# A two-block transformer kernel: the inputs of the RWKV scan made inside the attention's block and in the scan's first rounds, with sigmoids from exponential, plus one and reciprocal

## The chip, the cores and the metric

One core of one Trainium2 chip. The metric is the device time of one execution, in microseconds (us).

## The reference

The program runs two transformer blocks over 512 tokens of width 1024. The change touches the mixer of the first block. Its input projection gives queries, keys and values of eight attention heads and, after a token shift, `zr`: receptance, key and value of eight RWKV heads (64 wide each) and three low-rank inputs `xw`, `xa`, `xg`. The RWKV part computes:

```
kk = hs(k * k_k)
kk = kk * lax.rsqrt(jnp.maximum(jnp.sum(kk * kk, axis=-1, keepdims=True), 1e-12))
for direction in range(2):
    w = -softplus(-(w_decay0[direction] + jnp.tanh(xw) @ w_decay_up[direction])) - 0.5
    decay = jnp.exp(-jnp.exp(w))
    a = sigmoid(a_gate0[direction] + xa @ a_gate_up[direction])
    k_dir = k * (1.0 + (a - 1.0) * k_a)
    ys.append(wkv7_scan(hs(r), hs(decay), hs(k_dir), hs(v), kk, hs(a), reverse=(direction == 1)))
```

With s = sigmoid(w_decay0 + tanh(xw) @ w_decay_up) the decay is exp(-exp(-0.5) s), so the kernel keeps s itself, and two sigmoids are wanted for each direction: s (the "decays", tile `decay_sig`) and a (the "rates", tile `a`). The scan is a recurrence over the tokens. A product-key expert layer, a second mixer and a second expert layer follow; they are not changed.

## The kernel before, in words

Each stage is one block of programs, one for each engine, and all engines meet between blocks. The stages around the change are, in order: `stage_shifted` (projection and token shift), `stage_attention` (L687), `stage_rwkv_inputs` (L1005), `stage_rwkv_scan` (L1081) and `stage_rwkv_output` (L1515). Everything is f32, and the order of work on each engine is written out by hand; waits are on semaphore counts.

**Attention.** There are 32 units u: two heads by four tiles of 128 queries for each of four pairs of heads. TensorE makes scores for two units at a time (L730), VectorE adds a bias that SyncE streams from memory (L792) and takes the row maximum of the unit before (L795), ScalarE raises (L816) and copies the transposed probabilities (L808), TensorE transposes (`turn`, L739) and multiplies by the values (`mix`, L749). Four score tiles go round, so VectorE can be up to four units ahead of TensorE's transposes. After every eight units VectorE scales the rows (`scale`, L783 and L785), TensorE turns them back (L757) and ScalarE stores them (L812). GpSimd has nothing to do. Bank 7 of the accumulation memory is used by `turn_out` alone.

**Inputs.** In a block of its own: VectorE multiplies the keys (L1068), ScalarE squares them (L1039), TensorE sums them over each head (L1055), VectorE clamps (L1075). TensorE makes 16 products, one for each (direction d, pair of heads f, decay or rate), over 128 rows of which 64 are zero (L1062), and ScalarE evaluates Sigmoid straight from the bank (L1043). At the end ScalarE takes a logarithm (L1046) and an exponential (L1049) for the inverse root, and VectorE scales the keys (L1078).

**Scan.** There are eight rounds n; round n takes the pair of heads n // 2, forwards when n is even and backwards when it is odd. A round begins with four transposes (`turn`, L1377, copied by ScalarE at L1341) and five products (`gram`, L1389), then inverts triangular matrices in five levels l (`level` on VectorE, L1214; `z_products` and `w_products` on TensorE, L1406 and L1408; copies on ScalarE, L1349 to L1354), and ends with `end_products` and `gains` (L1247). Between these stand the 14 half steps of the recurrence of the round before (`chain`) and its output products. VectorE prepares round n + 1 in the levels of round n, one `prelude` part after each level (L1166 to L1191). In round 0 there is no chain; VectorE and GpSimd first copy unit matrices (L1262, L1266, L1310).

Of the kernel before, what the change touches and what calls it, by code (L numbers as in the profile page):

```python
# [25 lines left out]
P = 128  # L26
# [660 lines left out]
def stage_attention(core, qk, v, att):  # L687
# [9 lines left out]
    with ExitStack() as st:  # L697
        bias = core.sb("att_bias", [P, BIASES, TT, S], ctx=st)
# [11 lines left out]
        with nc.Block() as block:  # L710
            @block.sync
            def _(sp):
                core.clear_used(sp)
                for h in range(HEADS):
                    if h >= BIASES:
                        before = h - BIASES
                        sp.wait_ge(biased, PAIR * (before // 2) + PAIR - 1 + before % 2)
                    sp.dma_start(bias[:, h % BIASES, :, :], core.dram["att_bias"][h, :, :, :]).then_inc(bias_loaded[h % BIASES], 16)
                for j in range(BIASES):
                    sp.wait_ge(bias_loaded[j], 16 * len(range(j, HEADS, BIASES)))  # L720

            @block.tensor
            def _(pe):
# [28 lines left out]
                def turn_out(p):  # L752
                    pe.wait_ge(scaled, p + 1)
                    if p >= 1:
# [7 lines left out]
                for g in range(len(GROUPS)):  # L762
                    for h in range(2):
# [4 lines left out]
                        if u >= 2:  # L768
                            mix(u - 2)
                    if g % TT == 2 and g >= TT:  # L770
# [6 lines left out]
            def _(dve):  # L777
# [8 lines left out]

                for u, (h, i) in enumerate(UNITS):
# [5 lines left out]
                    if u >= 1:  # L793
                        dve.wait_ge(biased, u)
                        dve.tensor_reduce(top[:, u - 1:u], score[:, (u - 1) % SCORES, :], AX.X, ALU.max, negate=True).then_inc(topped, 1)  # L795
                    if u % PAIR == 3 and u >= PAIR:
# [6 lines left out]
            def _(act):  # L803
# [9 lines left out]

                for u in range(N):
# [3 lines left out]
                    if u >= 1:  # L818
                        copy_turned(u - 1)
                    if u % PAIR == 6 and u >= PAIR:  # L820
                        store(u // PAIR - 1)
                copy_turned(N - 1)
                store(HEADS // 2 - 1)
# [50 lines left out]
def first_block(core, first, mixed):  # L874
    with ExitStack() as st:
        zr = core.sb("zr", [P, 14, S], ctx=st)
        with ExitStack() as s2:
# [9 lines left out]
            stage_attention(core, qk, v, mixed)  # L887
        stage_rwkv(core, zr, mixed)
# [100 lines left out]
def stage_rwkv(core, zr, mixed):  # L989


    nc = core.nc
    R, K, V = 0, 4, 8
    with ExitStack() as st:
        sig = core.sb("decay_sig", [P, 8, S], ctx=st)
        a = core.sb("a", [P, 8, S], ctx=st)
        kk = core.sb("kk", [P, 4, S], ctx=st)
        sel = core.sb("rwkv_cols", [P, 4, 6], ctx=st)
        restart = core.sb("restart", [P, S], ctx=st)
        stage_rwkv_inputs(core, zr, sig, a, kk, sel, restart)  # L1000
        stage_rwkv_scan(core, zr, sig, a, kk, sel, restart, mixed)
        stage_rwkv_output(core, zr, a, sel, mixed)


def stage_rwkv_inputs(core, zr, sig, a, kk, sel, restart):  # L1005

    nc = core.nc
    with ExitStack() as st:

        lora = core.sb("lora", [P, 2, 2 * S], ctx=st)  # L1010
        low = core.sb("low", [P, S], ctx=st)
        sq = core.sb("kk_sq", [P, 4, S], ctx=st)
        lora_zeroed, loaded, restart_loaded, squashed, bank_full, emptied, made, squared, kk_full, clamped, logged, inverted = core.sems(
            st, "lora_zeroed", "lora_loaded", "restart_loaded", "squashed", "bank_full", "emptied", "kk_made", "squared", "kk_full", "clamped", "logged",
            "inverted")
        UNITS = [(d, f, which) for d in range(2) for f in range(4) for which in range(2)]
        NB = 4
        with nc.Block() as block:
            @block.sync
            def _(sp):  # L1020
                core.clear_used(sp)
                sp.dma_start(lora[0:HD, 0, :], core.dram["decay_up"]).then_inc(loaded, 16)
# [2468 lines left out]
```

## Time and profile before

| | |
|---|---|
| time, median of 3 runs | 2838.0 us (2835.01 to 2838.73) |
| the profiled execution's own time | 2833.37 us |
| its span | 2831.6 us |
| TensorE busy | 2392.0 us (84%) |
| VectorE busy | 1559.2 us (55%) |
| ScalarE busy | 982.1 us (35%) |
| attention | 259.4 to 338.4 us of the span |
| inputs of the scan | 338.7 to 368.6 us |
| scan | 368.9 to about 622 us |

Times in rows count from the start of the span. PE is TensorE, PEld its weight loads, DVE VectorE, ACT ScalarE, POOL GpSimd, SP SyncE (a name with q is the engine's sequencer). An f32 matmul is recorded as two, so one 128x128x512 product is "x2".

### The profile page before, as it was taken

How to read it: one execution, taken by the hardware profiler on the slowest of the kernel's cores; microseconds unless marked ns; L12 is line 12 of the kernel's file. 1: busy time of each engine (PE TensorE's matmuls, PEld its weight loads, DVE VectorE, ACT ScalarE, POOL GpSimd, SP SyncE). 2: the span in 40 equal slices, each digit the busy share in tenths (PEclk: the TensorE clock that was granted, in tenths of full speed). 3: DMA queues.
4: the chain of work that ended last, by engine and by line, in shares of the span. 5: the costliest groups of instructions: out<-in, count | busy, mean ns of one | idle time of the engine just before them, and what ended most of it. 6: DMA issues, size and time to landing. Idle time of an engine off the chain costs nothing. (4 is left out here: it accounts for less than half of the span.)

```text
span 2831.6 us, 45663 instructions
## 1 busy us (share of the span) xinstructions
PE 2392.0 (84%) x17210; PEld 1377.7 (49%) x17210; DVE 1559.2 (55%) x3601; ACT 982.1 (35%) x2559; POOL 927.2 (33%) x757
## 2 busy tenths in 40 slices
PE   6998979988899997777777777777779979889996
PEld 3544679985645443322233232322248878643333
DVE  6665555544666666666676766766554463420002
ACT  2121643324333333332333333333244332443333
POOL 0000021003244444555545555555520152223331
PEclk9999989998999999999999999999999966889998
DMA  9942100003499999999999999999942310379994
GB/s 374 375 166 96 59 13 4 5 4 123 181 398 398 385 384 410 421 421 419 418 416 414 415 416 411 419 409 416 417 180 82 119 39 2 125 285 357 376 355 172
DMA packets 174636, 770.15 MB, mean 272 GB/s; under 512 B 33728, under 2 KB 51792, under 8 KB 95056
## 3 DMA queue, kind: packets, MB, share of 16 engines
q0 software_dynamic: 87552, 545.34, 47.5%
q1 hardware_dynamic: 68176, 183.94, 17.5%
q10 hardware_dynamic: 18688, 37.95, 3.7%
q8 instruction: 137, 2.24, 0.3%
q14 instruction: 83, 0.68, 0.1%
HBM read 815.37 MB, written 16.78 MB: 294 GB/s over the span
## 5 line engine op out<-in xcount | busy, mean ns | idle before, releaser
L2126 PE MATMUL bank<-expert_rows,diagonals 128*128 128x512 f32 x1656 | 783.1, 611 | 210.3 <-ACT diagonals L2018 209.6
L1912 POOL DMA_INDIRECT expert_rows<-in_uv,expert_idx x414 | 533.6, 1289 | 576.8 <-PE bank L2126 476.2
L1947 DVE SCALAR_TENSOR_TENSOR expert_rows<-expert_rows,h_rows 128x1024 f32<-128x1024 f32 x414 | 507.4, 1225 | 343.6 <-DMA expert_rows<-in_uv,expert_idx 343.6
L2126 PEld LDWEIGHTS bank<-expert_rows,diagonals 128*128 128x128 f32 x1656 | 302.0, 192 | 639.1 <-ACT diagonals L2018 345.8
L2007 ACT ACTIVATE expert_act<-expert_dot 128x2 f32<-128x2 f32 x256 | 52.0, 203 | 865.4 <-DVE expert_rows L1947 662.2
L2126 PE MATMUL bank<-weight_slots,diagonals 128*128 128x512 f32 x392 | 180.8, 604 | 59.0 <-ACT diagonals L2018 59.0
L2018 ACT ACTIVATE diagonals<-ident,expert_weight 128x128 f32<-128x128 f32 x512 | 173.5, 386 | 0.0
L1947 DVE SCALAR_TENSOR_TENSOR weight_slots<-weight_slots,h_rows 128x1024 f32<-128x1024 f32 x98 | 120.1, 1225 | 89.6 <-DMA weight_slots<-in_uv,expert_idx 87.2
L1912 POOL DMA_INDIRECT weight_slots<-in_uv,expert_idx x98 | 132.6, 1354 | 109.4 <-issue 62.0
L594 DVE TENSOR_TENSOR w_lo<-weight_slots,w_hi 128x384 fp32r<-128x384 f32 (+3 forms) x120 | 80.7, 678 | 129.4 <-ACT w_hi L545 129.1
L2126 PEld LDWEIGHTS bank<-weight_slots,diagonals 128*128 128x128 f32 x392 | 70.6, 189 | 167.1 <-ACT diagonals L2018 89.8
L662 PE MATMUL bank<-rhs_hi,w_lo 128*128 128x512 f32 (+1 forms) x312 | 127.1, 407 | 23.2 <-DVE w_lo L594 15.2
L3448 DVE TENSOR_TENSOR hidden<-hidden,bank 128x256 f32<-128x256 f32 x24 | 10.1, 421 | 243.8 <-ACT hidden L3305 243.8
L2012 ACT ACTIVATE expert_weight<-expert_act,expert_gate 128x1 f32<-128x1 f32 x512 | 122.8, 287 | 8.6
L662 PE MATMUL bank<-rhs_lo,w_hi 128*128 128x512 f32 (+1 forms) x312 | 123.9, 397 | 0.0
L662 PE MATMUL bank<-rhs_hi,w_hi 128*128 128x512 f32 (+1 forms) x312 | 123.8, 397 | 0.0
L545 ACT ACTIVATE w_hi<-weight_slots 128x384 fp32r<-128x384 f32 (+3 forms) x120 | 63.5, 531 | 147.3 <-PE bank L662 145.9
L1030 POOL MEMSET lora<- 64x1024 f32 x1 | 0.9, 946 | 338.2 <-POOLq L710 338.2
L3206 PE MATMUL bank<-expert_w,tokens_turned 128*64 128x512 f32 x448 | 105.9, 608 | 0.7 <-ACT tokens_turned L3299 0.7
L925 PE MATMUL bank<-mixed,weight_slots 128*128 128x512 f32 x224 | 102.0, 611 | 0.6 <-PEq L405 0.3
L2069 PE MATMUL bank<-mixed,weight_slots 128*128 128x384 f32 x256 | 98.0, 489 | 0.0
L313 DVE SCALAR_TENSOR_TENSOR mod_acc<-mod_w,cond,mod_acc 128x512 f32<-128x512 f32 x144 | 97.4, 745 | 0.0
(531 smaller groups left out, 3974.3 us busy)
## 6 DMA issues: line engine op xcount, KB each, us to landing
expert_w<-in_experts SPq DMA_DIRECT2D x55, 1024.0 KB
expert_w_more<-in_experts SPq DMA_DIRECT2D x41, 1024.0 KB
mod_w<-in_ada_w ACTq DMA_DIRECT2D x17, 2048.0 KB, 11.8
mod_w<-in_ada_w SPq DMA_DIRECT2D x7, 2048.0 KB, 16.1
weight_slots<-in_w_in SPq DMA_DIRECT2D x6, 2048.0 KB, 17.9
weight_slots<-in_w_in SPq DMA_DIRECT2D x8, 1536.0 KB, 6.6
att_bias<-in_att_bias SPq DMA_DIRECT2D x8, 1024.0 KB, 6.2
weight_slots<-in_w_out SPq DMA_DIRECT2D x4, 2048.0 KB, 8.6
```

Source lines behind the costliest of these rows:

```text
L313: dve.scalar_tensor_tensor(out=a, in0=w, scalar=c, in1=a, op0=ALU.mult, op1=ALU.add).then_inc(self.weighed, 1)
L545: act.activation(w_hi[:, c % CH, 0:w.shape[2]], w[:, k, :], ACT.Copy).then_inc(w_upper, 1)
L594: dve.tensor_tensor(w_lo[:, c % CH, 0:w.shape[2]], w[:, k, :], w_hi[:, c % CH, 0:w.shape[2]].bitcast(F32), ALU.subtract).then_inc(w_split, 1)
L662: mm = pe.matmul(out, a, b, start=k == 0 and j == 0, stop=k == KD - 1 and j == 2)
L925: mm = pe.matmul(core.bank[u % NB][:, :], w[:, k, (u % 4) * P:(u % 4) * P + P], h[:, k, :], start=k == 0, stop=k == KD - 1)
L1912: pool.indirect_dma_start(rows[j], None, core.dram["uv"], bass.IndirectOffsetOnAxis(idx[:, t, column:column + 1], 0)).then_inc(arrived[j], 16)
L1947: dve.scalar_tensor_tensor(out=u, in0=u, scalar=1.0, in1=hN[:, t, :], op0=ALU.mult, op1=ALU.mult, accum_out=dot[:, j:j + 1]).then_inc(dott ...
L2012: act.activation(weight[:, j + i:j + i + 1], act_out[:, j + i:j + i + 1], ACT.Identity, scale=gates[:, t, column + i:column + i + 1]).then ...
L2018: act.activation(diag[:, j + i, :], core.ident[:, :], ACT.Identity, scale=weight[:, j + i:j + i + 1]).then_inc(diagonal, 1)
L2069: return pe.matmul(unit_bank(u)[:, 0:S - P], w[:, k, f * P:f * P + P], h2[:, k, P:S], start=k == 0, stop=k == KD - 1)
L2126: mm = pe.matmul(bank[2 * (t % 2) + half][:, :], diag[:, j, :], rows[slot_of(n)][:, D + half * S:D + half * S + S], start=column == 0, sto ...
L3206: mm = pe.matmul(gate_up_bank[n % 2][mine(half), :], tok[:, n % 2, k, mine(half)], both[half][:, k % HALF * S:k % HALF * S + S], start=k = ...
```

## The change

`stage_rwkv` and `stage_rwkv_inputs` are gone. A class `RwkvInputs` holds their tiles through attention and scan and gives each engine a few instructions to place between its own. The bias tiles of the attention lie in the slots of the weight ring, which are free there.

- In attention: before the first unit, keys, squares and the low-rank inputs (`first_on_vector`, `first_on_scalar`), beside three more loads on SyncE. At units 1 to 4 TensorE sums a square into bank 7, and VectorE clamps it at the unit after. At units 5 to 12 TensorE makes the eight products of pairs 0 and 1 into the same bank, one a unit, now over 64 rows with nothing to zero, and ScalarE raises each (exp of minus the sum) one unit later. At units 8 to 15 VectorE finishes the four of pair 0: plus one on even, reciprocal on odd ones. ScalarE takes the logarithm before its last store.
- In the scan: ScalarE begins with the four inverse roots, VectorE scales the keys (`norm_key`) around the unit matrices. In round 0 TensorE puts the other eight products behind the transposes (three behind the first, then two, two and one) and ScalarE raises them. In rounds 0, 2 and 4 VectorE has, after each of levels 0 to 3, one plus-one and one reciprocal of 128x512 (`squash`), for the next pair of heads.

```diff
...
     return evac
-def stage_attention(core, qk, v, att):
+def stage_attention(core, qk, v, att, rw):
...
     with ExitStack() as st:
-        bias = core.sb("att_bias", [P, BIASES, TT, S], ctx=st)
+        lent = core.ring.slots[:, :, :].rearrange("p r n -> p (r n)")
+        bias = lent[:, 0:BIASES * TT * S].rearrange("p (b i t) -> p b i t", b=BIASES, i=TT)
         score = core.sb("score", [P, SCORES, S], ctx=st)
...
                     sp.dma_start(bias[:, h % BIASES, :, :], core.dram["att_bias"][h, :, :, :]).then_inc(bias_loaded[h % BIASES], 16)
+                    if h == BIASES - 1:
+                        rw.load(sp)
                 for j in range(BIASES):
                     sp.wait_ge(bias_loaded[j], 16 * len(range(j, HEADS, BIASES)))
+                rw.all_loaded(sp)
             @block.tensor
...
                     pe.wait_ge(scaled, p + 1)
+                    if p == 0:
+                        pe.wait_ge(rw.raised, len(rw.EARLY))
                     if p >= 1:
...
                             mix(u - 2)
+                        rw.on_tensor(pe, u)
                     if g % TT == 2 and g >= TT:
...
+                rw.first_on_vector(dve)
                 for u, (h, i) in enumerate(UNITS):
...
                         dve.tensor_reduce(top[:, u - 1:u], score[:, (u - 1) % SCORES, :], AX.X, ALU.max, negate=True).then_inc(topped, 1)
+                    rw.on_vector(dve, u)
                     if u % PAIR == 3 and u >= PAIR:
...
+                rw.first_on_scalar(act)
                 for u in range(N):
...
                         copy_turned(u - 1)
+                    rw.on_scalar(act, u)
                     if u % PAIR == 6 and u >= PAIR:
...
                 copy_turned(N - 1)
+                rw.last_on_scalar(act)
                 store(HEADS // 2 - 1)
...
 def first_block(core, first, mixed):
-    with ExitStack() as st:
+    with ExitStack() as st, ExitStack() as held:
         zr = core.sb("zr", [P, 14, S], ctx=st)
...
                 stage_shifted(core, first + 3, h, zr, qk, m)
-            stage_attention(core, qk, v, mixed)
-        stage_rwkv(core, zr, mixed)
+            rw = RwkvInputs(core, held, zr, mixed)
+            stage_attention(core, qk, v, mixed, rw)
+        stage_rwkv_scan(core, zr, rw, mixed)
+        stage_rwkv_output(core, zr, rw.a, rw.sel, mixed)
...
+class RwkvInputs:
+    EARLY = [(d, 0, which) for d in range(2) for which in range(2)] + [(d, 1, which) for d in range(2) for which in range(2)]
+    LATE = [(d, f, which) for f in (2, 3) for d in range(2) for which in range(2)]
+    PAIRS, KK_AT, UNIT_AT, SIGMOID_AT = 4, 1, 5, 8
+    BANK, LATE_BANKS = 7, (4, 5, 6)
+    def __init__(self, core, st, zr, mixed):
+        self.core, self.zr = core, zr
...
+        self.low, self.sq = core.root, mixed[:, 4:8, :]
...
+    def product(self, pe, ps, unit):
+        d, f, which = unit
+        half = slice(HD * which, HD * which + HD)
+        at = d * S + f * P
+        return pe.matmul(ps[:, :], self.lora[half, at:at + P], self.low[half, :], start=True, stop=True)
+    def raise_unit(self, act, ps, unit):
+        d, f, which = unit
+        at = 8 * which + 4 * d + f
+        return act.activation(self.dest(unit), ps[:, :], ACT.Exp, scale=-1.0, bias=self.neg[:, at:at + 1])
+    def add_one(self, dve, unit):
+        return dve.tensor_scalar(self.dest(unit), self.dest(unit), 1.0, None, ALU.add)
+    def invert(self, dve, unit):
+        return dve.reciprocal(self.dest(unit), self.dest(unit))
+    def first_on_scalar(self, act):
+        act.activation(self.low[0:HD, :], self.zr[0:HD, 12, :], ACT.Tanh).then_inc(self.squashed, 1)
+        act.activation(self.low[HD:P, :], self.zr[HD:P, 12, :], ACT.Copy).then_inc(self.squashed, 1)
+        for f in range(4):
+            act.wait_ge(self.made, f + 1)
+            act.activation(self.sq[:, f, :], self.kk[:, f, :], ACT.Square).then_inc(self.squared, 1)
+    def first_on_vector(self, dve):
+        core, sel = self.core, self.sel
+        for f in range(4):
+            dve.tensor_scalar(self.kk[:, f, :], self.zr[:, 4 + f, :], core.col("k_k", f), None, ALU.mult).then_inc(self.made, 1)
+        dve.tensor_scalar(self.neg[:, :], core.col("w_decay0", 0, 16), -1.0, None, ALU.mult).then_inc(self.negated, 1)
...
+    def on_tensor(self, pe, u):
+        ps = self.core.bank[self.BANK]
+        f, i = u - self.KK_AT, u - self.UNIT_AT
+        if 0 <= f < 4:
+            pe.wait_ge(self.squared, f + 1)
+            if f >= 1:
+                pe.wait_ge(self.clamped, f)
+            pe.matmul(ps[:, :], self.core.headones[:, :], self.sq[:, f, :], start=True, stop=True).then_inc(self.kk_full, 1)
+        if 0 <= i < len(self.EARLY):
+            if i == 0:
+                pe.wait_ge(self.clamped, 4)
+                pe.wait_ge(self.loaded, 32)
+                pe.wait_ge(self.squashed, 2)
+            else:
+                pe.wait_ge(self.raised, i)
+            self.product(pe, ps, self.EARLY[i]).then_inc(self.unit_full, 1)
+    def on_scalar(self, act, u):
+        i = u - self.UNIT_AT - 1
+        if 0 <= i < len(self.EARLY):
+            if i == 0:
+                act.wait_ge(self.negated, 1)
+            act.wait_ge(self.unit_full, i + 1)
+            self.raise_unit(act, self.core.bank[self.BANK], self.EARLY[i]).then_inc(self.raised, 1)
+    def on_vector(self, dve, u):
+        f, i = u - self.KK_AT - 1, (u - self.SIGMOID_AT) // 2
+        if 0 <= f < 4:
+            dve.wait_ge(self.kk_full, f + 1)
+            dve.tensor_scalar(self.sq[:, f, :], self.core.bank[self.BANK][:, :], 1e-12, None, ALU.max).then_inc(self.clamped, 1)
+        if 0 <= i < 4:
+            if (u - self.SIGMOID_AT) % 2 == 0:
+                dve.wait_ge(self.raised, i + 1)
+                self.add_one(dve, self.EARLY[i]).then_inc(self.plus_one, 1)
+            else:
+                dve.wait_ge(self.plus_one, i + 1)
+                self.invert(dve, self.EARLY[i]).then_inc(self.squashed_units, 1)
+    def last_on_scalar(self, act):
+        act.wait_ge(self.clamped, 4)
+        act.activation(self.sq, self.sq, ACT.Ln)
+def stage_rwkv_scan(core, zr, rw, mixed):
...
     nc, bank = core.nc, core.bank
+    sig, a, kk, sel, restart, sq = rw.sig, rw.a, rw.kk, rw.sel, rw.restart, rw.sq
     R, K, V = 0, 4, 8
...
+        late_bank = lambda i: bank[rw.LATE_BANKS[i % len(rw.LATE_BANKS)]]
+        LATE_TURN = ((), (0, 1, 2), (3, 4), (5, 6), (7,))
         rev_of = lambda n: n % 2
...
                     decay = sig[:, 4 * d + f, :]
+                    if part == 0 and f >= 1:
+                        dve.wait_ge(squashed, 4 * f)
                     if part == 0:
...
                     elif part == 3:
+                        dve.wait_ge(kk_ready, f + 1)
                         dve.wait_ge(raised, 4 * n + 1)
...
+                def squash(n, l):
+                    f = pair_of(n) + 1
+                    if rev_of(n) == 0 and f < rw.PAIRS and l < 4:
+                        i = 4 * (f - 1) + l
+                        unit = (rw.EARLY + rw.LATE)[4 * f + l]
+                        if f >= 2:
+                            dve.wait_ge(late_raised, 4 * (f - 2) + l + 1)
+                        rw.add_one(dve, unit).then_inc(plus_one, 1)
+                        dve.wait_ge(plus_one, i + 1)
+                        rw.invert(dve, unit).then_inc(squashed, 1)
+                def norm_key(f):
+                    dve.wait_ge(inverted_kk, f + 1)
+                    dve.tensor_tensor(kk[:, f, :], kk[:, f, :], sq[:, f, :], ALU.mult).then_inc(kk_ready, 1)
                 prelude(0, 0)
...
                 prelude(0, 2)
+                norm_key(0)
                 dve.wait_ge(tables, 48)
...
                     dve.tensor_copy(units(t), tiled(eye[:, :], 2 * TT)).then_inc(gram_out, 1)
+                for f in range(1, rw.PAIRS):
+                    norm_key(f)
                 dve.wait_ge(gram_out, 6)
...
                             prelude(n + 1, l)
+                        squash(n, l)
                         if l < 2:
...
                         pool.wait_ge(z_full, 2 * NL * (n - 1) + 1)
+                    pool.wait_ge(kk_ready, f + 1)
+                    if f >= 1:
+                        pool.wait_ge(squashed, 4 * f)
                     pool.tensor_tensor(beta, a[:, 4 * d + f, :], kk[:, f, :], ALU.mult).then_inc(ops_pool, 1)
...
+                for f in range(rw.PAIRS):
+                    act.activation(sq[:, f, :], sq[:, f, :], ACT.Exp, scale=-0.5).then_inc(inverted_kk, 1)
                 decays(0, 0)
...
                         act.activation(to, bank[TURN_BANK[j]][:, :], ACT.Copy).then_inc(turn_out, 1)
+                        for i in LATE_TURN[j + 1] if n == 0 else ():
+                            act.wait_ge(late_full, i + 1)
+                            rw.raise_unit(act, late_bank(i), rw.LATE[i]).then_inc(late_raised, 1)
                     act.wait_ge(xs_full, n + 1)
...
                         turn(n, j)
+                        for i in LATE_TURN[j + 1] if n == 0 else ():
+                            if i >= len(rw.LATE_BANKS):
+                                pe.wait_ge(late_raised, i - len(rw.LATE_BANKS) + 1)
+                            rw.product(pe, late_bank(i), rw.LATE[i]).then_inc(late_full, 1)
+                        if n == 1 and j == 0:
+                            pe.wait_ge(late_raised, len(rw.LATE))
                         chain(n - 1, j)
...
```

## Rows read from the trace of the kernel before

**Rows 1.** Windows: busy us of PE, PEld, DVE, ACT, POOL; granted clock, DMA share.

```profile
280.00:300.00 20.00, 19.33 (x159) 13.94 (x158) 11.94 (x21) 13.39 (x31) 0.00 (x0) 1.00 0.38 141
...
389.10:401.00 11.90, 11.86 (x390) 11.62 (x386) 8.20 (x17) 5.81 (x21) 2.75 (x2) 1.00 0.02 4
...
448.80:462.80 14.00, 14.00 (x476) 13.92 (x474) 8.19 (x23) 5.71 (x21) 1.30 (x1) 1.00 0.02 5
```

**Rows 2.** Timeline of the inputs: start, us, instruction [idle before <- releaser].

```profile
337.81 0.60 ACT L812 ACTIVATE mixed<-bank 128x512 f32<-128x512 f32 x1 [2.87 <-PE bank L757]
...
338.71 3.14 DVE L1068 TENSOR_SCALAR kk<-zr,vec 128x512 f32<-128x512 f32 x4 [1.65 <-PEq L710]
...
346.27 13.90 PE L1062 MATMUL bank<-low,lora 128*128 128x512 f32 x32
...
360.91 1.28 ACT L1046 ACT_TABLE_LOAD   x1
362.20 1.91 ACT L1046 ACTIVATE kk_sq<-kk_sq 128x2048 f32<-128x2048 f32 x1
...
365.43 2.19 ACT L1049 ACTIVATE kk_sq<-kk_sq 128x512 f32<-128x512 f32 x4
...
368.89 1.23 DVE L1166 TENSOR_TENSOR_SCAN rwkv_work<-restart,decay_sig 128x512 f32<-128x512 f32 x1 [0.30 <-PEq L1018]
```

**Rows 3.** Reciprocals on VectorE by shape: total us, mean ns of one.

```profile
L1785 DVE RECIPROCAL gate_den<-gate_den 128x1 f32<-128x1 f32 x32 | 5.0, 155 | 0.0
L1920 DVE RECIPROCAL root<-root 128x128 f32<-128x128 f32 x4 | 3.8, 946 | 3.7 <-ACT root L1972 3.7
...
L3353 DVE RECIPROCAL token_root<-token_root 128x4 f32<-128x4 f32 x1 | 0.2, 178 | 1.3 <-ACT token_root L3279 1.3
```

**Rows 4.** Timeline of attention, VectorE and ScalarE on one unit.

```profile
308.67 0.68 DVE L792 TENSOR_TENSOR score<-bank,att_bias 128x512 f32<-128x512 f32 x1
308.79 0.72 ACT L816 ACTIVATE score<-score,top 128x512 f32<-128x512 f32 x1 [1.50 <-DVE top L795]
309.27 0.68 DVE L795 TENSOR_REDUCE top<-score 128x1 f32<-128x512 f32 x1
...
309.66 0.66 PE L739 MATMUL bank<-ident,score 128*128 128x128 f32 x4 [0.19 <-ACT score L816]
```

**Rows 5.** Timeline of attention, one period of two units.

```profile
302.60 0.66 PE L739 MATMUL bank<-ident,score 128*128 128x128 f32 x4 [0.17 <-ACT score L816]
...
303.19 1.09 PE L730 MATMUL bank<-qk 64*64 64x512 f32 x8
...
304.21 1.10 PE L749 MATMUL bank<-v,probT 128*128 128x64 f32 x8
...
306.76 0.66 PE L739 MATMUL bank<-ident,score 128*128 128x128 f32 x4 [0.16 <-ACT score L816]
```

**Rows 6.** Timeline of attention: unit 1's maximum, unit 5's transpose, unit 16's maximum.

```profile
269.50 0.68 DVE L795 TENSOR_REDUCE top<-score 128x1 f32<-128x512 f32 x1
...
280.12 0.61 PE L739 MATMUL bank<-ident,score 128*128 128x128 f32 x4
...
300.06 0.68 DVE L795 TENSOR_REDUCE top<-score 128x1 f32<-128x512 f32 x1
```

**Rows 7.** Timeline of the scan's head.

```profile
374.34 2.65 DVE L1262 COPY rwkv_work<-rwkv_eye 128x512 f32<-128x512 f32 x3 [0.39 <-DMA rwkv_eye<-in_rw_eye]
...
378.05 4.97 PE L1377 MATMUL bank<-ident,rwkv_work 64*64 64x64 f32 x96 [7.19 <-DVE rwkv_work L1185]
...
384.45 0.73 DVE L1197 COPY_PREDICATED rwkv_work<-rwkv_picks,bank 128x512 f32<-128x512 uint32 x1 [2.17 <-PE bank L1389]
```

**Rows 8.** Windows of the scan: as rows 1; the second of TensorE alone.

```profile
378.00:383.00 5.00, 4.95 (x102) 4.95 (x104) 4.28 (x5) 1.19 (x2) 5.00 (x7) 0.56 0.01 3
...
403.00:404.00 1.00, 1.00 (x20) 0.50 0.07 16
```

**Rows 9.** Timeline of VectorE, round 2's last level.

```profile
462.69 0.29 DVE L1214 TENSOR_TENSOR weight_slots<-bank,rwkv_masks 128x128 f32<-128x128 f32 x1 [2.50 <-PE bank L1408]
```

More of the change, by code:

```diff
@@ L986, in _ @@
                 m.finish(dve, m.NEEDED, m.ITEMS, [1, 2, 3])
[L989 to L1002, printed above, removed]
@@ L1081, in stage_rwkv_scan, with dest, load, all_loaded @@
-def stage_rwkv_scan(core, zr, sig, a, kk, sel, restart, mixed):
+class RwkvInputs:
[5 more added lines that the diff above has]
+        self.core, self.zr = core, zr
+        right = lambda name, shape: core.sb(name, shape, ctx=st, side="right")
+        self.sig = right("decay_sig", [P, 8, S])
+        self.a = right("a", [P, 8, S])
+        self.kk = right("kk", [P, 4, S])
+        self.sel = right("rwkv_cols", [P, 4, 6])
+        self.restart = right("restart", [P, S])
+        self.lora = right("lora", [P, 2 * S])
+        self.neg = right("neg_bias", [P, 16])
+        self.low, self.sq = core.root, mixed[:, 4:8, :]
+        (self.loaded, self.restart_loaded, self.negated, self.squashed, self.made, self.squared, self.kk_full, self.clamped, self.unit_full, self.raised,
+         self.plus_one, self.squashed_units) = core.sems(
+            st, "lora_loaded", "restart_loaded", "neg_made", "squashed", "kk_made", "squared", "kk_full", "clamped", "unit_full", "unit_raised",
+            "plus_one", "units_squashed")
+    def dest(self, unit):
+        d, f, which = unit
+        return (self.sig, self.a)[which][:, 4 * d + f, :]
+    def load(self, sp):
+        dram = self.core.dram
+        sp.dma_start(self.lora[0:HD, :], dram["decay_up"]).then_inc(self.loaded, 16)
+        sp.dma_start(self.lora[HD:P, :], dram["a_up"]).then_inc(self.loaded, 16)
+        sp.dma_start(self.restart[:, :], dram["rw_restart"]).then_inc(self.restart_loaded, 16)
+    def all_loaded(self, sp):
+        sp.wait_ge(self.loaded, 32)
+        sp.wait_ge(self.restart_loaded, 16)
+    def product(self, pe, ps, unit):
[4 more added lines that the diff above has]
+    def raise_unit(self, act, ps, unit):
+        d, f, which = unit
+        at = 8 * which + 4 * d + f
[15 more added lines that the diff above has]
+        dve.tensor_scalar(self.neg[:, :], core.col("w_decay0", 0, 16), -1.0, None, ALU.mult).then_inc(self.negated, 1)
+        for i, name in ((0, "k_a"), (3, "r_k"), (4, "lnx_g"), (5, "lnx_b")):
+            dve.tensor_copy(sel[:, :, i], core.col(name, 0, 4))
+        dve.tensor_scalar(sel[:, :, 1], core.col("k_a", 0, 4), -1.0, 1.0, ALU.mult, ALU.add)
+        dve.tensor_scalar(sel[:, :, 2], core.col("k_a", 0, 4), 0.5, None, ALU.mult)
+    def on_tensor(self, pe, u):
[36 more added lines that the diff above has]
+        act.activation(self.sq, self.sq, ACT.Ln)
@@ L1117, in stage_rwkv_scan @@
             "rw_u_full", "rw_u_out", "rw_s_full", "rw_state_out", "rw_held_out", "rw_y_full", "rw_y_copied", "rw_y_added")
+        late_full, late_raised, plus_one, squashed, inverted_kk, kk_ready = core.sems(
+            st, "rw_late_full", "rw_late_raised", "rw_plus_one", "rw_squashed", "rw_inverted_kk", "rw_kk_ready")
+        late_bank = lambda i: bank[rw.LATE_BANKS[i % len(rw.LATE_BANKS)]]
+        LATE_TURN = ((), (0, 1, 2), (3, 4), (5, 6), (7,))
         rev_of = lambda n: n % 2
```

68 lines of the change are left out of this document (removed).

## The prediction

> **What bounds the kernel here.** I read three views: windows over the stages, the timeline of each engine inside them, and the instructions by shape. In attention TensorE is busy 19.33 of 20 us while VectorE works 11.94, and in the levels of a scan round TensorE is busy 14.00 of 14.00 us and VectorE 8.19 [rows 1]. So VectorE has 5.8 us to spare in the four level steps of a round, and 4 us in ten in attention; TensorE has next to nothing. The inputs' block stands alone between the two: its engines wait for each other and nothing of attention or scan runs beside it [rows 2]. Whoever moves its work out of it wins that block, and pays wherever the work lands on TensorE, lands on VectorE beyond its spare time, or makes one engine wait for another that is behind it. All three occur here.
>
> **What goes.** ScalarE's last store of attention ends at 338.41, the next block's first instruction starts at 338.71, and the scan's first at 368.89 [rows 2]. Without the block the scan starts 0.3 after attention's end, so 368.89 - 338.71 = **30.2 us go**.
>
> **The price of a reciprocal.** 16 reciprocals of 128x512 come in, which the trace doesn't have. It has 128x1 at 0.155, 128x4 at 0.178 and 128x128 at 0.946 us [rows 3]. From 1 to 128 elements this is 6.2 ns an element, so 512 take 0.946 + 384 x 0.0062 = **3.34 us**, five times an addition of that shape (0.68 [rows 4]). Bounds: the 0.68 us of any other pass of 512 elements below, and above the slope of the two shortest, 7.7 ns, which gives 4.1. I take the value on the line, since its last point is by far the nearest. Plus-one is a one-input pass, 0.47 to 0.6; with the wait between the two a pair costs **3.85 us** of VectorE.
>
> The Trainium skill (VectorE: DVE Perf Modes, First, the fixed hardware budget) has the reciprocal iterate its divide with a repeat count of 8, which at the 0.96 GHz of its Specifications would be 8.3 ns an element and 4.3 us; the row of 128 elements gives 6.2 ns. By the page the sum below would be some 15 us higher.
>
> **Attention.** *Before unit 0* nothing is lost: the key products, tanh, squares and small columns run where VectorE and ScalarE wait for the first bias tile, until 265; the three more loads are issued behind three bias tiles and before SyncE would wait for unit 7.
>
> *The four round trips.* Read the two loops together. VectorE's clamp of sum f comes in its unit f + 2, just behind the maximum of unit f + 1. TensorE makes sum f in its unit f + 1, behind the transpose of that unit, which needs ScalarE's exponential, which needs that same maximum. So VectorE, which otherwise runs up to four units ahead, stands for a full trip round three engines, four times in a row. One trip: maximum 0.68; exponential and accumulator 0.87 until the transpose can start (308.79 to 309.66 [rows 4]); transpose 0.59; on every other trip scores 1.02; mix about 0.95 [rows 5]; sum 0.87 (13.90 / 16 [rows 2]) and 0.2 to its reader; clamp 0.69; addition 0.60. That is 5.5, or 6.5 with scores. The first starts at 270.2, where unit 1's maximum ends [rows 6]; TensorE's slow transposes and scores after it are there already, and the first clamp ends at 275.1. The next three end at 281.6, 287.2 and 293.8. Then unit 5's maximum 1.3, exponential 1.0: TensorE turns unit 5 at 296.15 against 280.12 [rows 6], **16.0 us late**.
>
> *The products and the reciprocals.* TensorE now has eight products of 0.87, 7 us. VectorE: units 6 to 8 at 1.2 (addition and maximum start 0.60 apart [rows 4]) until 297.5; it waits for the first raised product until 299.5; then plus-one, seven units, three more plus-ones, four reciprocals and the scaling of the rows: 0.5 + 8.4 + 1.5 + 13.4 + 0.9 = 24.7, to 324.2; units 16 and 17 2.4 more. So unit 16's maximum ends at 326.6 against 300.74 [rows 6], and TensorE, before it 1.9 behind VectorE and now 1.0, turns it at 327.6 against 302.60 [rows 5]: **25.0 us late** in all. Here VectorE bounds, by only 2 us over TensorE. Behind unit 16 all is as before. At the end the logarithm with its table load, 1.28 + 1.91 from 334.93, would end 0.3 after the store could start [rows 2]. Attention: **+25.2**. Bounds: +10.4, if the trips cost nothing but their twelve products, to +34, if TensorE runs them at half clock.
>
> **The scan's head.** ScalarE's table load and four exponentials (1.28 + 2.19 [rows 2]) run while VectorE does the first prefix sums, some 3.8. The Trainium skill (ScalarE: Activation LUTs, What ACT_TABLE_LOAD costs) adds a drain of 1.38 us to each load's 1.28; here the logarithm starts at 362.20, 0.01 after its load [rows 2], so I add none; by the page the head would be 1 us later. The first scaled key (0.69) stands where VectorE waits 0.39 for the unit matrices [rows 7], and before it the prefix sum is freed of GpSimd's product beside it; the other three (2.1) fill most of the 2.17 us that VectorE waits for the first `gram` product [rows 7]. GpSimd's first product starts 6 us later than it did, still before its reader.
>
> TensorE's three late products behind the first transpose lie in its idle 7.19 us [rows 7]. The other five stand between transposes that before took 4.97 us without a gap, on TensorE's own chain: 5 x 0.87 = 4.35, and 0.5 more because the first two may meet the low clock granted there, 0.56 between 378 and 383 [rows 8]. **+4.9**, bounds 4.4 to 8.
>
> **The levels.** A level step is: VectorE masks, TensorE multiplies, ScalarE copies, TensorE multiplies. The other work of VectorE, the `prelude` parts and pieces of the chain, runs beside this. The four steps from level 0 to level 4 take 14.0 us in round 2, with VectorE busy 8.19, and 11.9 in round 0, with 8.20 [rows 1]; at level 4 VectorE has waited 2.50 us for TensorE [rows 9]. `squash` puts 3.85 us behind the `prelude` part of each of the four, and the next mask stands behind it in VectorE's order, so once VectorE is the later one its work simply adds up:
> - Rounds 2 and 4: 8.19 + 4 x 3.85 = 23.6 against 14.0, **+9.6 each**. A step becomes 5 to 7 us, longer than TensorE's 3 to 4 with its copies, so VectorE sets all four.
> - Round 0: 8.20 + 15.4 = 23.6 against 11.9, 11.7; I take **+11**, as some of the 8.20 is VectorE slowed by a GpSimd product that will fall elsewhere.
> - Rounds 1, 3, 5 to 7: no `squash`, no change.
>
> Sum +30.2, less 0.5 a round as TensorE then finds its second half ready: **+28.7**. Bounds: +2, if a reciprocal took 0.68 (a pair of 1.2 fits in the spare time but for the first steps), to +38 with 4.1.
>
> **TensorE's clock.** With VectorE setting the pace TensorE pauses for 2 to 3 us in each trip and step. The granted clock fell to 0.50, the 1.2 GHz level, at 403 to 404 us [rows 8], right after short waits in round 0's last levels. In the trips half clock costs up to 2 us each, beside VectorE's reciprocals little, after the last level of a round about 1. I take half of the four trips and the ends of the rounds: **+4**, bounds 0 to 18.
>
> **Sum.** -30.2 + 25.2 + 4.9 + 28.7 + 4 = 32.6, some **+32** as the pieces' overlaps are dropped. The profiled execution took 2833.4 us by its own time, 1.8 over its span, and would take 2865; the median of the runs is 4.6 above that execution, so I predict **2870 us**.
>
> **Rivals.**
> - *Reciprocals fit in VectorE's idle time* (the other side). One mechanism: a 128x512 reciprocal costs like any pass of its width. In the levels it decides: below about 1.3 us a pair stays within the spare 5.8 us. Then levels +2, attention bound by trips and products +23, clock 0: -30.2 + 23 + 4.9 + 2 = 0: 2838. If the trips overlapped too it would be 2825. For it: 55% idle VectorE. Against: the 128x128 row. Chance 7%.
> - *The trips don't serialise*: VectorE finds the sums in time. Attention then costs twelve products, 10.4: -14.8, so 2855. Against it stand the positions in the loops. 10%.
> - *Half clock throughout the slow stretches*: 18 in place of 4, 2884. For it: rows 8; against: TensorE is still busy more than half of each trip. 13%.
> - *Reciprocal above the line* (4.1): 16 x 0.77 = 12 more, 2882. 8%.
>
> The forecast itself, 2858 to 2881, has 62%. A measurement of this kernel can tell 0.2%, 5.7 us. The range 2852 to 2886 leaves out the first rival and the tails. Slower 0.91, within 0.2% 0.05, faster 0.04.
>
> **What would show it.** Reciprocals of 3.3 us; the four clamps 5.5 to 6.5 us apart, each behind a wait for TensorE; unit 16's transpose 68 us after attention's start at 259.4 where it was 43; no gap between attention and scan; levels 5 to 7 us apart in rounds 0, 2 and 4 with TensorE waiting for VectorE, unchanged in the odd ones. A reciprocal under 1.3 us, or clamps 2 us apart, would make it wrong.

## The result, and the profile after

The changed kernel takes 2883.2 us in the median of four runs (2881.22 to 2894.13), against 2836.5 of the kernel before on the same chip (four runs): ratio 1.0174, 95% interval 1.016 to 1.0188. It is slower by some 47 to 49 us where +32 was forecast (2870, range 2852 to 2886); the time lies in the stated range, near its upper end, and above the 2858 to 2881 that the prediction called the forecast itself.

The profiled execution has a span of 2883.4 us (2885.17 by its own time). The page's first line shows that VectorE has 54 us more to do, and that TensorE, with as many matmuls as before (17210 records), is recorded busy for 47 us more:

```profile
PE 2438.9 (85%) x17210; PEld 1409.4 (49%) x17210; DVE 1613.7 (56%) x3634; ACT 980.5 (34%) x2558; POOL 922.8 (32%) x755
```

The time is found by cutting both spans at the same instructions: unit 0's addition in attention, the scan's first prefix sum, and `gains` at the end of a round (row starts in the timelines; the last column is the span less the start of round 7's `gains`). All the kernels of this study:

| kernel | up to unit 0 | attention (and inputs) | scan | its rounds 0, 2, 4 | rest |
|---|---|---|---|---|---|
| before | 265.1 | 103.8 | 251.6 | 38.6, 30.4, 30.4 | 2211.1 |
| changed | 264.6 | 114.2 | 288.1 | 54.2, 40.7, 41.0 | 2216.5 |
| e1_late_clamp | 266.3 | 86.1 | 293.0 | 54.5, 41.1, 45.5 | 2219.5 |
| e2_fill | 266.6 | 98.2 | 293.8 | 55.1, 45.6, 40.9 | 2210.8 |
| e3_att_plain | 264.6 | 110.1 | 292.7 | 54.3, 41.0, 45.5 | 2217.3 |
| e4_scan_plain | 266.5 | 114.3 | 260.7 | 47.0, 30.9, 30.9 | 2215.9 |
| e5_tanh | 266.6 | 110.1 | 254.0 | 40.9, 30.4, 30.4 | 2212.0 |
| e6_tanh_late | 267.6 | 85.3 | 257.0 | 43.5, 30.5, 30.4 | 2213.6 |
| e7_tanh_head | 264.8 | 81.2 | 254.0 | 41.3, 30.4, 30.4 | 2214.9 |
| e8_tanh_head_first | 266.2 | 82.1 | 252.7 | 39.8, 30.4, 30.4 | 2212.0 |

So the 51.8 us between the two spans are 10.4 in attention with the inputs' block gone, 36.5 in the scan, 5.4 behind it and -0.5 ahead. The work behind the scan was not changed, and that column lies between 2211 and 2220 over ten single executions, the first between 264.6 and 267.6. They are taken for scatter, though no run here was made to show it, and what is said of causes below rests on the two stages.

**Attention.** One of the four round trips, in the timeline of the changed kernel (L803 maximum, L826 exponential, L743 transpose, L753 mix, L1085 sum, L1107 clamp):

```profile
284.10 0.68 DVE L803 TENSOR_REDUCE top<-score 128x1 f32<-128x512 f32 x1
284.81 0.72 ACT L826 ACTIVATE score<-score,top 128x512 f32<-128x512 f32 x1 [6.72 <-DVE top L803]
...
285.67 1.12 PE L743 MATMUL bank<-ident,score 128*128 128x128 f32 x4 [2.82 <-ACT score L826]
286.58 1.81 PE L753 MATMUL bank<-v,probT 128*128 128x64 f32 x8
288.18 2.02 PE L1085 MATMUL bank<-mixed,headones 128*128 128x512 f32 x2
290.24 0.69 DVE L1107 TENSOR_SCALAR mixed<-bank 128x512 f32<-128x512 f32 x1 [5.47 <-PE bank L1085]
```

Read the brackets down the engines: ScalarE waited 6.72 us for VectorE, TensorE 2.82 for ScalarE, VectorE 5.47 for TensorE. Three engines take turns. The clamps start at 274.87, 282.89, 290.24 and 299.80: 8.0, 7.4 and 9.6 us apart where 6.5, 5.6 and 6.6 were forecast. The durations say why: transpose 1.12 where [rows 5] has 0.66, mix 1.81 for the 8 matmuls that [rows 5] shows in 1.10. The windows of TensorE alone (length, busy us, count, granted clock, DMA share, GB/s) from 270 to unit 5's transpose, on to 322, and to unit 16's transpose:

```profile
270.00:302.60 32.60, 21.32 (x75) 0.60 0.08 17
302.60:322.00 19.40, 19.40 (x64) 0.50 0.27 103
322.00:342.30 20.30, 20.14 (x130) 0.99 0.29 104
```

Attention before ran at 1.00 from 274. Here the mean over the four trips is 0.60: it came up to 1.00 near the end of TensorE's work in each of the first two trips, was 0.50 again by 278 and by 285, and from 285 to 322 it is 0.50, the 1.2 GHz level, without a break. Even after the trips, with TensorE recorded busy throughout, it stays there for 19 us.

**The reciprocals**, by tile (ns min/median/max), are as the line through [rows 3] said, 3.34 to 3.35 us:

```profile
L1059 DVE RECIPROCAL decay_sig<-decay_sig x8: 3341/3352/3353, 309.7 to 559.8; 128x512 f32<-128x512 f32 x8
L1059 DVE RECIPROCAL a<-a x8: 3343/3352/3354, 316.5 to 566.2; 128x512 f32<-128x512 f32 x8
```

**The scan.** Levels 0 to 4 of round 2 on VectorE, the answer to [rows 9]:

```profile
474.23 0.29 DVE L1263 TENSOR_TENSOR weight_slots<-bank,rwkv_masks 128x128 f32<-128x128 f32 x1
...
480.74 0.48 DVE L1263 TENSOR_TENSOR weight_slots<-bank,rwkv_masks 128x128 f32<-128x128 f32 x2
...
486.54 0.47 DVE L1263 TENSOR_TENSOR weight_slots<-bank,rwkv_masks 128x128 f32<-128x128 f32 x2
...
492.91 0.29 DVE L1263 TENSOR_TENSOR weight_slots<-bank,rwkv_masks 128x128 f32<-128x128 f32 x1 [0.92 <-PE bank L1484]
...
498.44 0.29 DVE L1263 TENSOR_TENSOR weight_slots<-bank,rwkv_masks 128x128 f32<-128x128 f32 x1
```

24.2 us from level 0 to level 4, 13.9 before. Of the four levels behind the first, three have no idle time in brackets: VectorE is late and TensorE waits for it. At 492.91 VectorE waited 0.92 for TensorE, which was at half clock.

### The profile page after: what moved, and what is told of

Same layout as the page of the kernel before. It is cut to its first block and busy times, and to the rows that moved or that the text cites. A ratio compares the mean times of both kernels' runs of the same rounds, so it can differ in the third digit from the quotient of the medians.

```text
span 2883.4 us, 45708 instructions
## 1 busy us (share of the span) xinstructions
PE 2438.9 (85%) x17210; PEld 1409.4 (49%) x17210; DVE 1613.7 (56%) x3634; ACT 980.5 (34%) x2558; POOL 922.8 (32%) x755
## 5 line engine op out<-in xcount | busy, mean ns | idle before, releaser
L2208 PE MATMUL bank<-weight_slots,diagonals 128*128 128x512 f32 x392 | 187.2, 622 | 57.8 <-ACT diagonals L2100 55.9
L1368 POOL TENSOR_TENSOR rwkv_work<-a,kk 128x512 f32<-128x512 f32 x8 | 10.2, 1274 | 486.7 <-DVE kk L1319 383.1
## 6 DMA issues: line engine op xcount, KB each, us to landing
expert_w<-in_experts SPq DMA_DIRECT2D x55, 1024.0 KB, 12.5
mod_w<-in_ada_w SPq DMA_DIRECT2D x7, 2048.0 KB, 16.1
```

The costliest lines, as they stand in the source:

```text
L2208: mm = pe.matmul(bank[2 * (t % 2) + half][:, :], diag[:, j, :], rows[slot_of(n)][:, D + half * S:D + half * S + S], start=column == 0, sto ...
```

## The experiments

Four kernels with one edit each to the changed kernel, each executed once, with a profile; then four with another sigmoid, executed four or five times each beside the kernel before, whose median there is 2834.5 us.

**e1_late_clamp** takes the round trips away.

```diff
     def on_vector(self, dve, u):
-        f, i = u - self.KK_AT - 1, (u - self.SIGMOID_AT) // 2
+        f, i = u - self.KK_AT - 3, (u - self.SIGMOID_AT) // 2
```

> One edit: VectorE clamps sum f in its unit f + 4 in place of f + 2; all else is as in the changed kernel. Measured is attention, from unit 0's addition to the scan's first prefix sum: 114.2 us in the changed kernel, 73.6 before without the inputs' block (103.8 less 30.2). Theory A (the four round trips, stretched by TensorE's half clock, are most of the growth of 40): VectorE no longer stands, attention falls to 86 to 93 us, TensorE turns unit 5 by 290 in place of 302.6, and the granted clock stays at 1.00 from about 275 on. Rival B (the reciprocals and plus-ones of units 8 to 15 are most of it): attention stays above 105. Whole kernel by A: 21 to 28 us less than the changed one; the scan is unchanged within 1 us.

Measured: attention 86.1 us; unit 5 is turned at 285.6; the clock is 0.50 until 276 (in the kernel before until 273) and 1.00 from 278 to 345. VectorE's waits for the four sums, 5.4 to 7.7 us in the changed kernel, have shrunk to 1.5 and less:

```profile
276.78 0.69 DVE L1107 TENSOR_SCALAR mixed<-bank 128x512 f32<-128x512 f32 x1 [1.41 <-PE bank L1085]
280.19 0.69 DVE L1107 TENSOR_SCALAR mixed<-bank 128x512 f32<-128x512 f32 x1 [1.52 <-PE bank L1085]
282.38 0.69 DVE L1107 TENSOR_SCALAR mixed<-bank 128x512 f32<-128x512 f32 x1 [0.31 <-PE bank L1085]
285.78 0.69 DVE L1107 TENSOR_SCALAR mixed<-bank 128x512 f32<-128x512 f32 x1 [1.52 <-PE bank L1085]
```

Theory A holds and B falls: 28 of attention's 40.6 us of growth (114.2 - 73.6) go though all four reciprocals are still there. The 12.5 that stay are what the twelve added products take on TensorE at 1.05 us from the start of one to the next instruction. Two parts of the expectation failed. The whole (2866.8 us in its one run) is 16 us below the changed kernel's median and 18.5 by the spans, not 21 to 28. And the scan was not within 1 us but 4.9 longer. Round 4 took 45.5 us where round 2, the same code, took 41.1. TensorE alone (busy us, count, granted clock), the last level steps and the end of round 2, then of round 4:

```profile
466.00:472.50 6.50, 6.50 (x148) 0.60 0.01 3
...
472.50:478.34 5.84, 5.46 (x184) 1.00 0.01 3
```

```profile
537.50:545.40 7.90, 7.90 (x154) 0.50 0.01 2
545.40:554.20 8.80, 8.42 (x176) 0.56 0.01 2
```

From level 0 to level 4 round 2 took 24.5 us and round 4 25.7, with the clock low for most of both; but behind level 4 the full clock was back in round 2, which ended after 5.6 us, and not in round 4, which took 8.8. While VectorE sets the pace the clock costs little; whether it is back when TensorE sets it again differs from one time to the next, and such a round loses 4 to 5 us. e2 lost them in round 2, e3 in round 4, the changed kernel in neither. The rest of e1's missing gain lies in the two columns outside the stages, 1.7 and 3.0 us.

**e2_fill** keeps the trips and changes the clock.

```diff
+                        if 2 <= u <= 5:
+                            pe.wait_ge(rw.clamped, u - 1)
+                        for _ in range(4 if u == 0 else 2 if 2 <= u <= 5 else 0):
+                            pe.matmul(bank[7][:, :], core.headones[:, :], rw.zr[:, 0, :], start=True, stop=True)
                         turn(u)
```

> TensorE gets filler products into the unused bank 7: four before the first transpose and two before each of the transposes of units 2 to 5, placed behind the wait for the clamp. The round trips stay. Theory A with the clock as a cause of its own: the granted clock in attention is near 1.00 from 270 to 322, where it was 0.50 to 0.71; clamps come 6 to 7 us apart in place of 7.4 to 9.6, and units 6 to 9 run at full clock; attention 114.2 -> 98 to 104 us. Rival C (the clock costs little, since VectorE or ScalarE would be late anyway): attention within 3 us of 114.2, or longer by the fillers. If the fillers do not raise the clock, it is 114 to 120 and the question stays open.

Measured: attention 98.2 us, 16.0 less, though TensorE has twelve products more. The whole is 2871.05 us in its one run, 12 below the changed kernel's median. The clamps, and the windows of TensorE from unit 0's addition to 300 and on to unit 16's transpose:

```profile
276.97 0.69 DVE L1111 TENSOR_SCALAR mixed<-bank 128x512 f32<-128x512 f32 x1 [5.42 <-PE bank L1089]
283.42 0.69 DVE L1111 TENSOR_SCALAR mixed<-bank 128x512 f32<-128x512 f32 x1 [4.57 <-PE bank L1089]
288.65 0.69 DVE L1111 TENSOR_SCALAR mixed<-bank 128x512 f32<-128x512 f32 x1 [3.35 <-PE bank L1089]
295.09 0.69 DVE L1111 TENSOR_SCALAR mixed<-bank 128x512 f32<-128x512 f32 x1 [4.56 <-PE bank L1089]
```

```profile
266.58:300.00 33.42, 25.39 (x106) 0.90 0.31 103
300.00:328.40 28.40, 28.28 (x179) 1.00 0.30 118
```

The clock was 0.50 from 270 to 276, so the four products ahead of the first transpose did not keep it up, and 1.00 from 278 on. The clamps are 6.5, 5.2 and 6.4 us apart, where the forecast had 6.5, 5.6 and 6.6. Work that serves nothing made the kernel faster, so the half clock was a cause of its own, and rival C falls. It also isolates the forecast's other terms: at full clock from the second trip on, attention with the inputs' block grows by 98.2 - 103.8 = -5.6 us, where -30.2 + 25.2 = -5.0 was worked out. What the four trips cost at that clock is the difference to e1, 98.2 - 86.1 = 12.1 us.

**e3_att_plain**

```diff
+    def plain(self, dve, unit):
+        return dve.tensor_scalar(self.dest(unit), self.dest(unit), 0.0, 0.5, ALU.mult, ALU.add)
...
-                self.invert(dve, self.EARLY[i]).then_inc(self.squashed_units, 1)
+                self.plain(dve, self.EARLY[i]).then_inc(self.squashed_units, 1)
```

> The four reciprocals inside attention are replaced by a multiply-add pass of the same tiles that writes 0.5, so the first pair's decays and rates are wrong; the 12 of the scan stay. Theory A: they lie beside TensorE's half-clock products and cost little of their own; attention 114.2 -> 110 to 114. Rival B (4 x 2.9 = 11.7 us of VectorE are on the path): attention about 102.

Measured: attention 110.1, inside what Theory A said, and 4.1 less than with the reciprocals. But the 4.1 are not VectorE's time. Unit 5 is turned 1.3 us later than in the changed kernel; then the full clock is back after 8 us of work without a pause, where it took 19.4 us:

```profile
303.90:312.00 8.10, 8.10 (x29) 0.50 0.62 246
312.00:322.00 10.00, 10.00 (x58) 0.99 0.00 0
```

From unit 5's transpose to unit 9's and on to unit 16's (us):

| kernel | reciprocals in attention | 5 to 9 | 9 to 16 |
|---|---|---|---|
| before | no | 8.3 | 14.2 |
| changed, e4 | yes | 21.5 | 18.2 |
| e3, e5 | no | 16.2 | 18.2 |
| e1, e2 | yes | 12.3 | 18.2 |
| e6, e7, e8 | no | 12.3 | 18.2 |

At full clock both stretches are as long with the reciprocals as without. TensorE sets them, and what is added to the kernel before is its products. So the four reciprocals, 11.7 us of VectorE, fit beside TensorE's work in attention. e3 and the changed kernel part already at unit 3, turned 1.3 us later in e3, before VectorE has any plus-one or reciprocal; that the clock came back sooner can't be put down to the edit by these runs.

**e4_scan_plain** has the same edit in `squash`: the 12 reciprocals of the scan are left out, those of attention stay.

> The 12 reciprocals inside the scan's rounds are replaced by a multiply-add pass that writes 0.5 (0.42 us in place of 3.35), so decays and rates of pairs 1 to 3 are wrong. Theory A (VectorE's work adds up once it is the later engine): level 0 to level 4 falls from 21.9 to 12 to 13 us in round 0 and from 24.2 to 14 to 15 in rounds 2 and 4; the scan's growth of 36.3 falls to 5 to 8, of which 4.7 is the head's. The whole is 28 to 31 us less. Rival D (the new waits and the plus-ones do it, whatever their length): no more than 10 us go.

Measured: the scan 260.7, so 27.4 of its 36.5 go with the 12 reciprocals. Level 0 to level 4 takes 14.4 us in round 0 and, in round 2, as before:

```profile
469.08 0.29 DVE L1266 TENSOR_TENSOR weight_slots<-bank,rwkv_masks 128x128 f32<-128x128 f32 x1
...
483.42 0.29 DVE L1266 TENSOR_TENSOR weight_slots<-bank,rwkv_masks 128x128 f32<-128x128 f32 x1 [1.70 <-PE bank L1487]
```

14.3 us, with VectorE waiting for TensorE again. The two short passes per level are nearly free in rounds 2 and 4 (30.9 against 30.4). Theory A holds; the 9.1 left are 1 more than expected, in round 0 (14.4 in place of 12 to 13). The whole, 2859.3 us in its one run, is 24 below the changed kernel's median and 26 by the spans, not 28 to 31.

**e5_tanh** keeps the result and drops the reciprocal.

```diff
-        return act.activation(self.dest(unit), ps[:, :], ACT.Exp, scale=-1.0, bias=self.neg[:, at:at + 1])
+        return act.activation(self.dest(unit), ps[:, :], ACT.Tanh, scale=0.5, bias=self.neg[:, at:at + 1])
...
-        return dve.tensor_scalar(self.dest(unit), self.dest(unit), 1.0, None, ALU.add)
+        return dve.tensor_scalar(self.dest(unit), self.dest(unit), 0.5, 0.5, ALU.mult, ALU.add)
...
-                        rw.add_one(dve, unit).then_inc(plus_one, 1)
-                        dve.wait_ge(plus_one, i + 1)
-                        rw.invert(dve, unit).then_inc(squashed, 1)
+                        rw.add_one(dve, unit).then_inc(squashed, 1)
```

The bias columns are made with 0.5 in place of -1, and the reciprocal in attention goes the same way.

> The same result by another identity: sigmoid(x) = 0.5 tanh(x / 2) + 0.5, so ScalarE evaluates Tanh in place of Exp (no other table) and VectorE makes one multiply-add pass (0.42 us) in place of plus-one and reciprocal (3.85). Everything else as in the changed kernel, the four round trips too. Theory A (trips and clock cost attention's growth, reciprocals the scan's): attention with the inputs' block, 103.8 us before and 114.2 in the changed kernel, is 109 to 113; the scan, 251.6 before and 288.1, is 257 to 261; so the whole is 11 to 18 us slower than before. Rival B (the reciprocals were the whole cost): attention about 90, the whole 5 us or more faster than before.

Measured: 2849.9 us (five runs), 15.4 over before, ratio 1.0055 (1.0036 to 1.0074). Attention 110.1; the scan 254.0, better than expected by 3, in round 0 (40.9 against e4's 47.0). So the scan's term goes with the reciprocals, and attention's stays.

**e6_tanh_late** is e5 with e1's clamps.

> e5 with the clamps two units later, as in e1. Theory A: the two causes are separate and add: attention 84 to 87, scan 257 to 261, the whole 8 to 14 us faster than before (ratio about 0.996). If the causes cover each other, less is gained than e1 and e4 gave together.

Measured: 2818.4 us, 16.1 below before and so a little better than expected, ratio 0.9943 (0.9923 to 0.9963); attention 85.3, scan 257.0. The two causes add: attention is 28.9 below the changed kernel where e1 was 28.1 below it, the scan 31.1 where e4 was 27.4.

**e7_tanh_head** is e5 with the four sums ahead of the first transpose.

```diff
                 scores(0)
+                rw.sum_on_tensor(pe, 0)
+                rw.sum_on_tensor(pe, 1)
                 scores(1)
+                rw.sum_on_tensor(pe, 2)
+                rw.sum_on_tensor(pe, 3)
```

`sum_on_tensor(f)` writes bank 4 + f; VectorE clamps sums 0 and 1 before unit 0, sums 2 and 3 in units 1 and 2; the first users of banks 4 to 6 wait for the clamps.

> e5 with the four sums of squares made into banks 4 to 7 before the first transpose, where TensorE waits some 7 us for the first maximum, and clamped before unit 0 (two) and in units 1 and 2. Theory A (TensorE bounds attention once nobody makes a trip, so only products that lie in its idle time are free): against e6 four products of 1.05 less, attention 81 to 84; the whole 11 to 17 us faster than before. If they delay the first transpose, up to 2 us more.

Measured: 2817.8 us, ratio 0.994 (0.9917 to 0.9962); attention 81.2 us, 4.1 less than e6, as four products of 1.05 say. The medians of e6 and e7 differ by 0.6 us alone, so the gain is seen in the stage and not in the whole.

**e8_tanh_head_first** is e7 with another order in the scan's head.

```diff
-        LATE_TURN = ((), (0, 1, 2), (3, 4), (5, 6), (7,))
+        LATE_TURN = ((), (0, 1, 2, 3, 4, 5, 6, 7), (), (), ())
```

> e7 with all eight late products behind the scan's first transpose, where TensorE was idle for 7.2 us before the second. Theory A (the head's 4.7 us are the five products that stand between the transposes): the scan's first round, 38.6 us before and 47 with the five between, becomes 43 to 45; ScalarE's eight raises of 0.6 after its first copy then end about 2 us after the second operand is ready. Rival: ScalarE's raises set it, wherever they stand, and the first round stays at 46 to 47.

Measured: 2813.3 us, ratio 0.9924 (0.9902 to 0.9945), the lowest median here. Round 0 is 39.8 us, 1.2 over before. The expectation had 43 to 45, counted from the 47 of e4; e7, which differs from e8 by this edit alone, has 41.3. Up to level 0 the head takes 21.1 us, 24.1 in e7 and 20.2 before: the products between the transposes were its cost, as Theory A says, and ScalarE's raises were not. Behind level 4 the round loses 1.5 of the 3 us again, 6.0 from the last mask to `gains` in place of 4.4. Two stretches of its timeline, attention's head and the scan's:

```profile
262.37 2.87 PE L1090 MATMUL bank<-mixed,headones 128*128 128x512 f32 x4 [0.28 <-ACT mixed L1076]
...
264.41 0.69 DVE L1094 TENSOR_SCALAR mixed<-bank 128x512 f32<-128x512 f32 x1 [1.82 <-PE bank L1090]
...
266.18 1.98 PE L1090 MATMUL bank<-mixed,headones 128*128 128x512 f32 x4
...
269.87 0.68 DVE L1094 TENSOR_SCALAR mixed<-bank 128x512 f32<-128x512 f32 x1
```

```profile
354.47 3.60 PE L1058 MATMUL bank<-root,lora 64*128 64x512 f32 x10 [0.97 <-ACT decay_sig L1063]
358.00 3.03 PE L1460 MATMUL bank<-ident,rwkv_work 64*64 64x64 f32 x96
```

The sums lie where TensorE waited for the first maximum, and the last clamps find them ready. In the scan the second to fourth transposes follow the late products without a gap and take 3.03 us for the 96 matmuls that took 4.97 in [rows 7]: TensorE, idle for 7.19 us there, now comes to them at full clock (1.00 from 354.5). The 1.9 us are not gained by the head, though: behind the `gram` products TensorE now waits 1.98 us for VectorE, which has the three scaled keys in front of its masks.

## Why the prediction was right in its direction and low in its size

Point by point, with the sum's own terms:

- *The inputs' block goes, -30.2.* Held: the scan's first prefix sum starts 0.3 us after attention's last store ends, 378.44 and 378.74 in the changed kernel.
- *Reciprocal 3.34 us.* Held, 3.34 to 3.35. A line through rows of 1 and 128 elements carried to 512. The Trainium skill (VectorE: DVE Perf Modes, First, the fixed hardware budget) gives the reciprocal's divide a repeat count of 8 and no duration; the estimate worked out from it, 4.3 us, doesn't agree with the trace, and the measured 3.34 decides. Plus-one took 0.42, not 0.47 to 0.6, so a pair costs 3.72 us and not 3.85.
- *Attention +25.2 at full clock* (trips 16.0 to unit 5, 25.0 to unit 16). The sum held to 1 us: in e2, unit 5 is turned 31.3 us after unit 0's addition and unit 16 61.9 after it, against 15.0 and 37.5 before: 16.3 and 24.4 late. Its parts did not all hold. From unit 5 on the prediction let VectorE with its reciprocals bound, 2 us over TensorE. TensorE bounds there, with or without them (the table under e3). A product costs it 1.05 us where 0.87 was taken, and so unit 16 comes 30.6 us after unit 5 (e2) where the forecast's VectorE needed 31.5; that the two lie so close is luck. Of attention's growth of 24.6 in e2 the twelve products are 12.5 (e1) and the trips 12.1.
- *The scan's head +4.9, levels +28.7.* Held: to level 0 the changed kernel takes 24.9 against 20.2, +4.7; levels +10.0 in round 0 (11 forecast) and +10.3 in round 2 (9.6 forecast). e4 shows that their length is the reciprocals'.
- *The clock, +4.* This is the step that failed. The forecast took half clock for half of the four trips and for the ends of rounds, and said that it costs little beside VectorE's reciprocals, since it had VectorE as the bound there. The trips cost 6.7 us by it (unit 5 turned 38.0 us after unit 0's addition, 31.3 in e2). Units 5 to 8 behind them cost 9.2 more (21.5 us against 12.3): TensorE had no pauses left, set the pace, and stayed at half clock. Unit 16 was turned 77.8 us after unit 0's addition, 15.9 more than in e2. In the scan the clock cost about 1 at the end of round 0. With 16 to 17 in place of 4, the sum is +45; with the 5.4 behind the scan, for which no cause is shown, it is 50 to 51 of the 51.8 between the spans.

The rival "half clock throughout the slow stretches", 2884 us at 13%, comes nearest; its 18 for the clock is nearly the term measured. In part that is luck too: it spoke of the stretches in which TensorE pauses, and more than half of what was measured fell on units 5 to 8, where it did not pause, and about 1 us on the scan. The chances were misplaced between it and the forecast. One of the signs that the prediction named failed with the clock: the clamps are 7.4 to 9.6 us apart, not 5.5 to 6.5. The other three rivals fall: the reciprocals don't fit in VectorE's idle time in the scan (e4), though they do in attention (e1 and e6); the trips do serialise (e1); and the reciprocal lies on the line.

What stays open: why the clock came back only at 322. In e3 and e5 TensorE does the same work in the same order behind the trips, and the full clock was back after 8 us; in e4 it took as long as in the changed kernel. No run here varies what TensorE does in units 5 to 8 with the trips unchanged.

## What to carry to other kernels

Work that is spread over another stage's loop must be placed by where each engine stands in that loop, not by its own numbering: a result that VectorE takes one unit after TensorE makes it costs a whole trip round the engines where VectorE could run up to four units ahead, and taking it two units later left only TensorE's own time for the products. A forecast for such a stretch needs the clock as a term of its own: here the four trips cost 12.1 us as waits and 15.9 more by half clock, 9.2 of it behind them. Price a reciprocal by its length before choosing an identity, and then ask which engine bounds where it stands: four cost nothing in attention, twelve cost 27 us in the scan. Tanh with one multiply-add pass gave the same sigmoid for a ninth of VectorE's time, and with it, a better placement of the sums and of the late products, the same change became 0.8% faster than the kernel before in place of 1.7% slower. Put added matmuls where TensorE waits: they are free there. What follows may also find the full clock: it did in e7's first units and in e8's scan, and did not in e8's first units, whose work from 272 to 274 met 0.50.

## What the runs showed of the hardware

- TensorE stayed at the 1.2 GHz level for 19.4 us in which its records are busy without a gap (302.6 to 322 in the changed kernel), behind 33 us of work with a pause of about 2.8 us in each trip. In e3, with the same work on TensorE, it stayed there for 8 us.
- Matmuls whose results nobody reads, put into TensorE's waits, took 16 us off attention (e2).
- The same round of the scan, paced by VectorE, took 41 or 45.5 us, from round to round of one execution, by whether the full clock was back when TensorE set the pace again.
- A product over 64 rows costs TensorE what one over 128 costs: at full clock, each alone between other work, the first lasts 1.12 us (L1048, units 9 to 12 of the changed kernel) and the second 1.08 (the sums of e2 from the second on). Halving the rows saved the zeroing, and no time on TensorE.
